# Fillers behind the band's scores, mixing in parts, rotation tables begun earlier and column norms in a transformer kernel

## The chip, the cores and the metric

The kernel runs on one core of a Trainium2 chip. Its time is device microseconds of one launch, and lower is better. TensorE (PE) multiplies, VectorE (DVE), ScalarE (ACT) and GpSimd (POOL) do elementwise work, SyncE (SP) starts the loads. The engines run their own queues in order and wait for each other by semaphores. TensorE's clock is granted at one of two levels, 1.2 GHz (0.50 in the views) and 2.4 GHz (1.00).

## The reference

512 tokens of width 1024 pass through two blocks. The first adds a mixer, a memory attention and an expert layer to the stream; the second (two layers, with a state-space mixer, a latent attention and a delta rule) is touched by the change only in its latent attention. The mixer, cut to what matters:

```python
proj = rmsnorm(h, norm_mix_g) @ w_in            # q, k, v of 8 heads of 64, and u
att = chunked_attention(rmsnorm(q), rmsnorm(k), v, rel_bias)
ssm = s5_mixer(u, ...)                          # x_t = a * x_{t-1} + B u_t, a = mag * exp(i * angle)
mixed = concat(rmsnorm(att, att_out_g), rmsnorm(ssm, ssm_out_g))
h = h + mixed @ w_out
# memory attention: k = rmsnorm(memn @ w_mem_k) per head of 256
```

Chunks of 64 queries see up to eight chunks of keys before them and their own, with a bias by distance. The state-space part is computed with tables of cos and sin of (angle x t) for all 512 t, `Er` and `Ei`, and a scan.

## The kernel before

Everything is float32. Activations lie transposed, 128 rows of a feature chunk by 512 tokens. Weight products are done as three products of a high and a low part (lines 103 to 105); `Weights` (line 430 on) loads a 128x1024 tile of weights, ScalarE makes its high part (L471), VectorE its low part (L483) two tiles ahead. `linears` runs a list of such products tile by tile; after tile i each engine also runs the step i of the norms given to it (`act_at`, `pe_at`, `dve_at`). `weights.filler` is a 128x128 tile of ones; `fill` (L458) issues products of it whose result nobody reads.

The first 0.7 ms run these stages in order, each closed by a barrier of all engines:

- mix_in (from 10 us): 16 tiles of w_in give q, k, v, u, with `GroupNorm` for q and k beside them (reciprocal of 128x512 on VectorE, L319) and `StateTables` on GpSimd, which computes the powers of the rotation (L1288 to 1292) and later, behind a small reciprocal of VectorE (L1266), the scaled C matrices. A turn of v (L809) follows.
- band attention (`attention`, L883; called at L1133): 32 jobs, 8 heads h by 4 blocks q of 128 queries, a job having (q+1) x 128 keys. In iteration j TensorE multiplies the scores of job j (L943), transposes the probabilities of job j-2 (L919), and, once a head's four jobs are turned, mixes the values of a whole head in one go (L932; L928 in the packed form of the latent attention), in iteration 4h+6. VectorE adds the bias (L973), takes the maximum (L976), and normalises job j-1 (L958, L962). ScalarE takes the exponential (L1009), copies the turned probabilities of j-2 (L995) and stores a head (L1000). GpSimd meanwhile doubles the rotation tables (`rotations`, L1322): from n known columns to 2n, for k = 0 to 8; in the last doubling ScalarE makes half the products (`act_aside`, L1341) in jobs 19 to 26, and waits at job 19 until k = 0 to 7 are done.
- state_space: 16 tiles, VectorE rotates and scans (L1398 to 1409), GpSimd rotates back (L1422 to 1425), both reading `Er` and `Ei`.
- gated unit, then mix_out: 8 tiles of w_mem_k and 8 of w_out. `GroupNorm` normalises the mixed stream (2 groups of 4 chunks) for the w_out tiles and the memory's k (4 groups of 2). For a group: squares (ACT), sums of the chunks (DVE, L315), one product with the tile of ones (PE, L304) that sums over rows and gives the sum on every row, root (ACT, L289), reciprocal (DVE, L319) and scaling (DVE, L322) over the whole width; then the high part (ACT, L294) and the low part (POOL, L327), for which the first w_out tile waits.
- mem_in, memory attention (L1183, two key tiles), mem_out, experts. Much later the latent attention runs twice (L2433), packed, with a gate's products between its jobs (`GateBeside`).

## Time and profile before

| | |
|---|---|
| time, median of 3 runs | 5266.63 us (5266.21 to 5267.07) |
| profiled execution, its own time | 5271.14 us |
| span of the profiled execution | 5269.4 us |
| TensorE busy | 4995.3 us (95%) |
| VectorE, ScalarE, GpSimd busy | 2956.7, 1774.7, 703.9 us (56%, 34%, 13%) |
| TensorE's granted clock, mean | 0.972 |

The profile lists one execution. Busy time of TensorE is modelled from pipelined products, so that differences of starts say more than durations. A row in order of time shows start, duration, engine, line, operation, output and inputs, a count where equal rows are merged, and in brackets the idle time before it with what ended it. A float32 product shows as two records.

### The profile page before, as it was taken

What the parts mean: (1) busy time and instruction counts of PE and PEld (TensorE: products, weight loads), DVE (VectorE), ACT (ScalarE), POOL (GpSimd) and SP (SyncE); (2) the same over time, 40 slices, a digit from 0 to 9 for tenths busy, and PEclk for the clock granted to TensorE, in tenths of its full rate; (3) what the DMA queues carried; (4) which work ended last, traced back from release to release, by engine and by line L of the source; (5) the groups of instructions that cost most, each with busy time, mean ns of one, the idle gap of its engine ahead of it and who ended that gap; (6) DMA issues with size and microseconds to landing.
All of it is one profiled execution on the core that took longest, in us unless ns stands there. A gap on an engine that the chain in (4) does not pass through costs nothing. (4 is left out here: it accounts for less than half of the span.)

```text
span 5269.4 us, 62000 instructions
## 1 busy us (share of the span) xinstructions
PE 4995.3 (95%) x23936; PEld 4012.4 (76%) x23936; DVE 2956.7 (56%) x5352; ACT 1774.7 (34%) x2720; POOL 703.9 (13%) x494
## 2 busy tenths in 40 slices
PE   8679899999999999999899998999999999989999
PEld 6227688888887888878887676888878876767887
DVE  6577558898403444465455465544565465566433
ACT  3314433333322322243333333343323333323422
POOL 3741002232240000001200001000003000011000
PEclk9799999999999999998999999999989999999999
DMA  2012123555546555530022020222210221212222
GB/s 105 24 42 86 53 103 118 184 185 185 182 152 217 192 192 192 195 113 24 1 96 84 33 88 32 104 96 96 90 43 1 83 70 56 72 45 96 92 98 82
DMA packets 231732, 527.57 MB, mean 100 GB/s; under 512 B 19600, under 2 KB 89488, under 8 KB 230032
## 3 DMA queue, kind: packets, MB, share of 16 engines
q1 hardware_dynamic: 231440, 523.61, 29.2%
q8 instruction: 192, 3.15, 0.2%
q14 instruction: 100, 0.82, 0.1%
HBM read 448.03 MB, written 75.50 MB: 99 GB/s over the span
## 5 line engine op out<-in xcount | busy, mean ns | idle before, releaser
L483 DVE TENSOR_TENSOR weight_low<-ring,weight_high 128x1024 fp32r<-128x1024 f32 (+2 forms) x606 | 710.4, 1173 | 1233.3 <-PE banks L105 1169.1
L471 ACT CAST weight_high<-ring 128x1024 fp32r<-128x1024 f32 (+2 forms) x728 | 729.1, 1003 | 540.8 <-PE banks L105 524.2
L103 PE MATMUL banks<-x_high,weight_high 128*128 128x512 f32 x1856 | 748.6, 403 | 30.0 <-DVE weight_low L483 17.0
L483 POOL TENSOR_TENSOR weight_low<-ring,weight_high 128x1024 fp32r<-128x1024 f32 x122 | 299.2, 2454 | 3302.9 <-PE banks L105 2146.6
L105 PE MATMUL banks<-x_high,weight_low 128*128 128x512 f32 x1856 | 728.8, 393 | 0.0
L104 PE MATMUL banks<-x_low,weight_high 128*128 128x512 f32 x1856 | 728.4, 392 | 0.0
L103 PEld LDWEIGHTS banks<-x_high,weight_high 128*128 128x128 f32 x1856 | 351.8, 190 | 143.2 <-issue 49.1
L103 PE MATMUL banks<-xn_high,weight_high 128*128 128x512 f32 x1024 | 411.0, 401 | 0.7 <-ACT hT L1638 0.7
L104 PEld LDWEIGHTS banks<-x_low,weight_high 128*128 128x128 f32 x1856 | 352.1, 190 | 75.4 <-issue 5.8
L105 PEld LDWEIGHTS banks<-x_high,weight_low 128*128 128x128 f32 x1856 | 351.4, 189 | 74.8
L103 PE MATMUL banks<-act_high,weight_high 128*128 128x512 f32 x1024 | 399.5, 390 | 5.6 <-DVE act_low L1870 5.6
L105 PE MATMUL banks<-xn_high,weight_low 128*128 128x512 f32 x1024 | 399.8, 390 | 0.0
L105 PE MATMUL banks<-act_high,weight_low 128*128 128x512 f32 x1024 | 399.1, 390 | 0.0
L104 PE MATMUL banks<-act_low,weight_high 128*128 128x512 f32 x1024 | 399.1, 390 | 0.0
L104 PE MATMUL banks<-xn_low,weight_high 128*128 128x512 f32 x1024 | 398.6, 389 | 0.0
L1841 ACT CAST act_high<-activations 128x512 fp32r<-128x512 f32 x126 | 78.8, 626 | 488.8 <-PE banks L105 484.9
L103 PEld LDWEIGHTS banks<-act_high,weight_high 128*128 128x128 f32 x1024 | 192.8, 188 | 46.4 <-issue 6.4
L105 PEld LDWEIGHTS banks<-xn_high,weight_low 128*128 128x128 f32 x1024 | 192.2, 188 | 41.5
L1749 DVE TENSOR_SCALAR first_hot<-iota,spare,rstd 128x128 f32<-128x128 f32 x512 | 185.2, 362 | 68.6 <-ACT rstd L1663 52.2
L104 PEld LDWEIGHTS banks<-act_low,weight_high 128*128 128x128 f32 x1024 | 192.8, 188 | 39.9
L105 PEld LDWEIGHTS banks<-act_high,weight_low 128*128 128x128 f32 x1024 | 192.7, 188 | 40.1
L103 PEld LDWEIGHTS banks<-xn_high,weight_high 128*128 128x128 f32 x1024 | 192.8, 188 | 36.1 <-ACT hT L1638 0.9
(616 smaller groups left out, 9127.5 us busy)
## 6 DMA issues: line engine op xcount, KB each, us to landing
ring<-in_peer_u SPq DMA_DIRECT2D x128, 512.0 KB, 3.4
ring<-in_peer_v SPq DMA_DIRECT2D x128, 512.0 KB, 3.4
acts<-dot_act SPq DMA_DIRECT2D x128, 256.0 KB, 2.0
gates<-gate_block SPq DMA_DIRECT2D x64, 512.0 KB, 6.1
ring<-in_w_up SPq DMA_DIRECT2D x64, 512.0 KB, 3.2
ring<-in_w_down SPq DMA_DIRECT2D x64, 512.0 KB, 3.2
activations<-acts SPq DMA_DIRECT2D x126, 256.0 KB, 3.7
gates_in<-gates SPq DMA_DIRECT2D x126, 256.0 KB, 3.9
```

The source lines that it names most:

```text
L103: nc.tensor.matmul(out, w_high, x_high, start=start, stop=False)
L104: nc.tensor.matmul(out, w_high, x_low, start=False, stop=False)
L105: return nc.tensor.matmul(out, w_low, x_high, start=False, stop=stop)
L471: self.nc.scalar.copy(self.wH[:, g % HIGHS, 0:kc * P], self.ring[:, g % SLOTS, 0:kc * P]).then_inc(self.high_made, 1)
L483: ops.tensor_tensor(self.wL[:, g % LOWS, 0:kc * P], self.ring[:, g % SLOTS, 0:kc * P], self.wH[:, g % HIGHS, 0:kc * P].bitcast(F32), ALU.s ...
L1749: v.tensor_scalar(hotA[:, m % HOTS, k, :], iota, first[:, n:n + 1], gateT[:, n:n + 1], ALU.is_equal, ALU.mult)
L1841: nc.scalar.copy(aH[:, n % 2, :], weighed_tile(n)).then_inc(act_high, 1)
```

## The change

1. **Fillers.** In each of the band's 32 jobs TensorE issues four products of the tile of ones into bank 7 behind the scores. Nobody reads them.
2. **Mixing in parts.** In all attentions a head's mixing is cut into parts (by key tile, or by query block in the packed form), one in each of the iterations from 4h+6 on. The store of a head moves back accordingly.
3. **Rotation tables.** The table is allocated before mix_in, as two halves of 256 columns. Doublings k = 0 to 5 are done by GpSimd in mix_in, right after the powers; 6 to 8 stay in the band attention. ScalarE's share of the last doubling moves from jobs 19 to 26 to jobs 13 to 20, with its wait. The input's high and low parts lie in the second half of the table until then; v's transpose moves into mixT and the tile of half-ones into vS. State_space reads both tables as 2 x 256 columns.
4. **Column norms.** mix_out's two norms become `ColumnNorm`: TensorE sums over rows with the data as weights and one column of ones, root and reciprocal are taken on 128 x 4 (or 128 x 2) elements, and TensorE spreads them over rows and columns with the identity. The scaling reads the result from PSUM. The first norm's groups follow each other one tile apart, no longer two.

The diff, cut to its core:

```diff
+class ColumnNorm(GroupNorm):
...
+        buffer, _, self.ident, columns, _ = tools
+        self.column, self.buffer, self.tiles = columns[:, 0:1], buffer, self.n // P
...
+    def root(self, g):
+        return self.buffer[:, g * self.tiles:(g + 1) * self.tiles]
...
+            self.nc.scalar.activation(self.root(g), self.bank(g)[:, 0:self.tiles], ACT.Sqrt, scale=1.0 / self.width, bias=self.eps)\
+                .then_inc(self.rooted, 1)
...
+    def pe_at(self, pe, i):
+        for g, chunks in self.at_step(i, 2):
+            pe.wait_ge(self.added, (g + 1) * (self.group - 1))
+            if g >= 3:
+                pe.wait_ge(self.scaled, (g - 2) * self.group)
+            for t in range(self.tiles):
+                last = self.nc.tensor.matmul(self.bank(g)[:, t:t + 1], self.scratch(chunks[0])[:, t * P:(t + 1) * P], self.column,
+                                             start=True, stop=True)
+            last.then_inc(self.summed, 1)
+        for g, chunks in self.at_step(i, 4):
+            pe.wait_ge(self.inverse, g + 1)
+            for t in range(self.tiles):
+                last = self.nc.tensor.matmul(self.bank(g)[:, t * P:(t + 1) * P], self.root(g)[:, t:t + 1].to_broadcast([P, P]), self.ident,
+                                             start=True, stop=True)
+            last.then_inc(self.spread, 1)
+
...
+        v = self.nc.vector
+        for g, chunks in self.at_step(i, 5):
+            dve.wait_ge(self.scaled, (g + 1) * self.group)
...
+        for g, chunks in self.at_step(i, 3):
+            dve.wait_ge(self.rooted, g + 1)
+            v.reciprocal(self.root(g), self.root(g)).then_inc(self.inverse, 1)
+        for g, chunks in self.at_step(i, 4):
+            dve.wait_ge(self.spread, g + 1)
+            for c in chunks:
+                v.scalar_tensor_tensor(self.y(c), self.x(c), self.gain(c), self.bank(g), ALU.mult, ALU.mult).then_inc(self.scaled, 1)
 
...
+MIXED_FROM = 6
+WARM = 4
+            def mix(h, part):
+                if part == 0:
+                    pe.wait_ge(copied, TT * (h + 1))
+                    if h >= 2:
+                        pe.wait_ge(stored, h - 1)
+                if packed:
+                    for k in range(part + 1):
+                        last = nc.tensor.matmul(banks[4 + h % 2][place(h), part * P:(part + 1) * P], values(h, k),
+                                                pt[:, h % 2, place_of(part) + k * P:place_of(part) + (k + 1) * P],
+                                                start=(k == 0), stop=(k == part))
+                elif part < keys(TT - 1):
+                    k = part
...
+            for j in range(len(jobs) + MIXED_FROM + TT):
...
+                    for _ in range(WARM if warm is not None else 0):
+                        nc.tensor.matmul(banks[7][:, 0:P], warm, warm, start=True, stop=True)
...
-                if j >= 3 and jobs[j - 3][1] == TT - 1:
-                    mix(jobs[j - 3][0])
+                h, part = divmod(j - MIXED_FROM, TT)
+                if 0 <= h < heads and part < parts:
+                    mix(h, part)
...
-                if j >= 4 and jobs[j - 4][1] == TT - 1:
-                    store(jobs[j - 4][0])
+                h, part = divmod(j - MIXED_FROM, TT)
+                if 0 <= h < heads and part == parts:
+                    store(h)
+                if 0 < h <= heads and parts == TT and part == 0:
+                    store(h - 1)
...
-                halves = mixT[:, 0, 0:P]
+                halves = vS[:, 2, 0:P]
...
+                vT = mixT[:, 0:4, :]
+                xH, xL = ssm.pair()
...
-                              aside=ssm, in_banks=True)
+                              aside=ssm, in_banks=True, warm=weights.filler)
...
-                    norm = GroupNorm(nc, chunks_of(mixT), chunks_of(mixT), 8, 4, tools, 512, lambda c: col("mixed_g", c), chunks_of(scratch),
-                                     banks, 0, 2, pair=pair)
+                    norm = ColumnNorm(nc, chunks_of(mixT), chunks_of(mixT), 8, 4, tools, 512, lambda c: col("mixed_g", c), chunks_of(scratch),
+                                      banks, 0, 1, pair=pair)
...
+        half = 4 * 2 * N * (T // 2)
+        self.x_at = [nc.sbuf_base + half + k * half // 2 for k in range(2)]
+        self.E = sb("turns", [P, 2, 2, N, T // 2])
+        self.first_half, self.second_half = self.E[:, 0], self.E[:, 1]
...
+        link(g.memset(self.first_half[:, 0, :, 0:1], 1.0))
+        link(g.memset(self.first_half[:, 1, :, 0:1], 0.0))
+        for k in range(self.EARLY):
+            self.double(g, link, k)
...
-    LAST = 8
+    EARLY, LAST, ACT_FROM = 6, 8, 13
...
+    def double(self, ops, link, k, before=None):
+        n, m = 1 << k, self.batch(k)
+        first = self.first_half
+        tmp = self.big[:, 0:m * n].rearrange("p (m n) -> p m n", n=n)
+        for t0 in range(0, SSM_TILES, m):
+            t = slice(t0, t0 + m)
+            c_, s_ = bc(self.power[:, k, 0, t], n), bc(self.power[:, k, 1, t], n)
+            if before:
+                before(t0 + m)
+            for which, op in ((0, ALU.subtract), (1, ALU.add)):
+                new = first[:, which, t, n:2 * n] if k < self.LAST else self.second_half[:, which, t, :]
+                link(ops.tensor_tensor(tmp, first[:, 1 - which, t, 0:n], s_, ALU.mult))
+                if k < self.LAST:
+                    link(ops.tensor_tensor(new, first[:, which, t, 0:n], c_, ALU.mult))
+                link(ops.tensor_tensor(new, new, tmp, op))
...
+        for k in range(self.EARLY, self.LAST):
+            self.double(ops, link, k)
+        self.double(ops, link, self.LAST, lambda tiles: eng.wait_ge(scaled, 2 * tiles))
...
+        k, j = self.LAST, j - self.ACT_FROM
+        if j == 0:
+            act.wait_ge(step, sum(6 * (SSM_TILES // self.batch(x)) for x in range(self.EARLY, k)))
+        for t in (2 * j, 2 * j + 1) if 0 <= j < SSM_TILES // 2 else ():
+            for which in range(2):
+                self.nc.scalar.activation(self.second_half[:, which, t, :], self.first_half[:, which, t, :], ACT.Copy,
+                                          scale=self.power[:, k, 0, t:t + 1]).then_inc(scaled, 1)
...
-                v.tensor_tensor(w[:, 0, :], b0, Er[:, i, :], ALU.mult)
...
+                v.tensor_tensor(w0, b0, Er(i), ALU.mult)
...
```

## Rows read from the trace of the kernel before

**Rows 1.** TensorE's rows in order of time, over one head of the band attention

```profile
145.50 1.12 PE L943 MATMUL banks<-qkT 64*128 64x512 f32 x2
...
148.85 0.55 PE L919 MATMUL banks<-ident,scratch 128*128 128x128 f32 x3 [1.44 <-DVE scratch L962]
...
150.23 0.66 PE L919 MATMUL banks<-ident,scratch 128*128 128x128 f32 x4 [0.20 <-DVE scratch L962]
...
152.32 3.56 PE L932 MATMUL banks<-ring,vS 128*64 128x512 f32 x8
155.81 1.12 PE L943 MATMUL banks<-qkT 64*128 64x512 f32 x2
156.86 0.44 PE L919 MATMUL banks<-ident,scratch 128*128 128x128 f32 x2
157.23 0.48 PE L943 MATMUL banks<-qkT 64*128 64x128 f32 x2
```

**Rows 2.** Busy time and count by engine, then PEclk, DMA share, GB/s, windows

```profile
149.50:152.00 2.50, 2.30 (x9) 0.92 (x9) 1.85 (x5) 2.25 (x7) 2.34 (x3) 0.87 0.00 0
152.00:154.50 2.50, 2.50 (x4) 0.85 (x5) 1.67 (x4) 0.92 (x4) 2.42 (x2) 0.50 0.01 3
154.50:157.00 2.50, 2.50 (x9) 1.00 (x8) 0.03 (x1) 0.00 (x0) 2.42 (x2) 0.95 0.00 0
```

**Rows 3.** ScalarE in the band attention, in order of time

```profile
168.72 0.69 ACT L1009 ACTIVATE banks<-scratch,spare 128x512 f32<-128x512 f32 x1 [4.29 <-DVE spare L976]
...
179.74 0.51 ACT L1348 ACTIVATE Er<-Er,power 128x256 f32<-128x256 f32 x1 [10.21 <-POOL Ei L1339]
...
219.61 0.69 ACT L1009 ACTIVATE banks<-scratch,spare 128x512 f32<-128x512 f32 x1 [4.65 <-DVE spare L976]
...
222.15 0.59 ACT L995 COPY ring<-banks 128x512 f32<-128x512 f32 x1 [0.62 <-PE banks L919]
...
226.89 0.58 ACT L1000 COPY mixT<-banks 64x512 f32<-64x512 f32 x1 [4.15 <-PE banks L932]
```

**Rows 4.** GpSimd in mix_in and the band attention, in order of time

```profile
105.61 0.22 POOL L1303 TENSOR_TENSOR ssm_par<-ssm_par 128x16 f32<-128x16 f32 x1 [38.29 <-DVE ssm_par L1266]
...
120.51 0.13 POOL L1325 MEMSET Er<- 128x16 f32 x1 [3.39 <-SPq L60]
...
141.55 1.90 POOL L1336 TENSOR_TENSOR scratch<-Ei,power 128x1024 f32<-128x1024 f32 x1
...
177.37 2.34 POOL L1339 TENSOR_TENSOR Ei<-Ei,scratch 128x1024 f32<-128x1024 f32 x1
```

**Rows 5.** VectorE and TensorE in mix_out, in order of time

```profile
402.12 3.35 DVE L319 RECIPROCAL scratch<-scratch 128x512 f32<-128x512 f32 x1
405.51 3.75 DVE L322 SCALAR_TENSOR_TENSOR mixT<-mixT,vec,scratch 128x512 f32<-128x512 f32 x4
409.18 2.29 DVE L483 TENSOR_TENSOR weight_low<-ring,weight_high 128x1024 fp32r<-128x1024 f32 x1
...
430.80 1.23 DVE L483 TENSOR_TENSOR weight_low<-ring,weight_high 128x1024 fp32r<-128x1024 f32 x1 [4.93 <-PE banks L105]
...
411.52 0.58 PE L103 MATMUL banks<-mem_high,weight_high 128*128 128x256 f32 x1 [5.27 <-DVE weight_low L483]
...
423.35 0.50 PE L103 MATMUL banks<-mixed_high,weight_high 128*128 128x512 f32 x1 [3.16 <-DVE weight_low L483]
```

**Rows 6.** Fillers at the end of mix_in; column sums in the last norm

```profile
113.75 2.17 PE L458 MATMUL banks<-ones 128*128 128x128 f32 x18
...
5255.36 1.95 PE L363 MATMUL banks<-columns,scratch 128*128 128x1 f32 x16 [1.38 <-DVE scratch L378]
```

**Rows 7.** TensorE in the memory attention and in the latent attention

```profile
571.64 0.44 PE L919 MATMUL banks<-ident,scratch 128*128 128x128 f32 x2 [0.35 <-DVE scratch L962]
571.91 1.03 PE L943 MATMUL banks<-qkT,mqT 128*128 128x256 f32 x4
...
2957.36 0.47 PE L103 MATMUL banks<-x_high,weight_high 128*128 128x512 f32 x1 [0.28 <-DVE gdn_v L855]
```

More of the change, by code:

```diff
@@ L933, in mix @@
                                             start=(k == 0), stop=(k == keys(TT - 1) - 1))
-                last.then_inc(mixed, 1)
-            for j in range(len(jobs) + 3):
+                if part == parts - 1:
+                    last.then_inc(mixed, 1)
+            for j in range(len(jobs) + MIXED_FROM + TT):
                 if j < len(jobs):
@@ L1000, in store @@
                 nc.scalar.copy(out(h), banks[4 + h % 2][place(h), :]).then_inc(stored, 1)
-            for j in range(len(jobs) + 4):
+            for j in range(len(jobs) + MIXED_FROM + TT + 1):
                 if j < len(jobs):
@@ L1127, in mix @@
+                linears(nc, "mix_in", [qk, Linear("mix_v", dram["w_in"], 8, 4, DC, x, scaled_to(vT, rstd)),
+                                       Linear("mix_u", dram["w_in"], 12, 4, DC, x, scaled_to(uT, rstd))],
+                        weights, banks, fold=fold, norms=[norm_qk, ssm], loads=ssm.loads)
+                turn(nc, "mix_v", chunks_of(vT), vS, 4, TT, banks, ident)
                 with tables:
[L1128 removed]
+                    ssm.turns(scratch)
```

120 lines of the change are left out of this document (56 added, 64 removed).

## The prediction

> **What bounds the kernel now.** The page first: TensorE is busy nearly throughout. So time can only be won where it waits, runs at the low clock, or does needless work, and everything the diff touches lies in the first 0.7 ms, apart from the order of the mixing in two later attentions. I read the stages there by windows, then engine by engine in order of time.
>
> The band attention (first scores just before 120.5 us, last copy out at 226.89 + 0.58 = 227.5) is the loose stage. One head is four jobs. In undisturbed stretches a head takes 155.81 - 145.50 = 10.31 us [rows 1]: VectorE and ScalarE have room, and TensorE loses 1.44 + 0.20 us waiting for normalised scores, and some more because its clock falls. The three windows that cover a head show a granted clock of 0.87, 0.50 and 0.95 [rows 2], so 2 x (0.13 + 0.50 + 0.05) x 2.5 = 3.4 us are at 1.2 GHz, which costs half of that, 1.7 us. The fall comes after a stretch with waits, and the long mixing product (3.56 us) then runs mostly at the low level [rows 1]. On top of that stands a stall: ScalarE waits 10.21 us for GpSimd's rotation tables, and the three heads from exponential 19 to exponential 31 take 219.61 - 168.72 = 50.9 us instead of 30.9 [rows 3]. GpSimd is the engine behind it: it starts at 120.51, and finishes the doublings k = 0 to 7 at 177.37 + 2.34 = 179.71 [rows 4].
>
> In mix_out the second bound shows: TensorE waits 5.27 and 3.16 us for weight_low, while VectorE does reciprocals of 3.35 us and scalings of 3.75 us ahead of it in its queue [rows 5].
>
> **Part 1, the doublings moved to the projection stage.** The six early ones took 141.55 - 120.51 = 21.0 us [rows 4] and now run inside mix_in, where GpSimd is idle for 38.29 us ahead of 105.61 [rows 4]. That idle time hides them; without it they would cost their 21 us. What remains before ScalarE may scale is k = 6 and 7: 179.71 - 141.55 = 38.2 us, so ready at 120.5 + 38.2 = 158.7 instead of 179.7. The last doubling (about 35 us) ends near 199, off the path. Price in mix_in: VectorE's subtraction L483 takes 1.23 us alone and 2.29 us beside GpSimd [rows 5], so up to 1.06 us for each of the three or four that meet the moved work, 4 us of delay at most, some of it regained, and the stage ends with GpSimd's chain behind VectorE's small reciprocal. Between 0 and 3 us; I take 0.5, because a product needs its weights only a tile later.
> The Trainium skill, "SBUF — State Buffer", section "SBUF: two separate sides", speaks against this move: a VectorE operation with two SBUF inputs and a GpSimd operation that reads SBUF exclude each other for a whole instruction. The 2.29 against 1.23 us agrees. If it held for every subtraction and every scaling beside the moved work, with none of it regained, the kernel would end 2.5 us later than I say.
>
> **Part 2, fillers and spread mixing in the band.** Each of 32 jobs gets four products of ones. Nine such products take 2.17 us [rows 6], 0.24 each with the last one's drain, so 16 a head cost about 3.7 us at the full clock. A head's other work at the full clock is 10.31 - 1.64 (waits) - 1.7 (low clock) = 7.0. So a head would take 7.0 + 3.7 = 10.7 us, with no wait left and the clock held: the fillers cost what the clock gives, and the steady pace does not improve (between 10.0, if switches between kinds of product overlap, and 11.3, if each filler group adds 0.15 us of switching; two transposes hold the next scores up for 157.23 - 156.86 = 0.37 us here and for 571.91 - 571.64 = 0.27 in the memory attention, so a switch can cost 0.1 and more [rows 1, 7]). The gain of the stage is the stall's. Walk: mixing is about 2.2 of the 10.7 and trails the scores by six jobs. Exponential 19 starts after five heads without mixing (5 x 8.5, less 1.5 that follows its scores) plus 3.4 heads' mixing (7.4), plus 1.4 on VectorE: 120.5 + 41.0 + 7.4 + 1.4 = 170.3; exponential 31 at 170.3 + 3 x 10.7 = 202.4, against 219.61 [rows 3].
> ScalarE reaches its wait at job 13 near 155 by the same count, so a stall of some 4 us stays; queued behind it are ScalarE's copies of turned probabilities, for which TensorE's transposes and mixing wait. Two jobs of slack absorb part of it, a fall of the clock in it costs something back: 0 to 6 us, I take 2.5. ScalarE's 16 scalings a head, at most 0.51 us each [rows 3], beside its own 3.2 us in 7.5 [rows 2], keep it at the same 10.7 us or slightly above for two heads. Exponential 31 then stands at 205. The tail was 7.9 us (219.61 to 227.5), with its mixing at the low clock; I take 7, so the stage ends at 212: **-15 us** (-8 to -21).
>
> **Part 3, ColumnNorm in mix_out.** Sums become one column and the inverse root is taken on 128x4 and spread by TensorE. VectorE loses two reciprocals of 3.35 us and four of half the width. Its scalings read the root from PSUM and no longer two SBUF tensors: 3.75 us for four becomes about 3.0. TensorE pays: 8 column products took 1.95 us [rows 6], so 4 cost 1.0, and four spreading products 4 x 0.24 = 1.0, against 0.9 for one product with ones: +1.1 for each of two wide groups and +0.55 for each of four narrow ones, 4.4 us. Walk: tile 2 still waits for the first sums to about 392. The four scalings of the first group, now behind a reciprocal and done at 409.2, run from about 403.8 to 407; the next subtraction follows a tile's end directly, so the 5.27 us wait goes, with the low clock behind it. Pace 1 instead of 2 brings the second group forward: scaled near 412.5, weight_low for the first w_out tile near 414.5 instead of 423.3 (TensorE starts at 423.35). That tile ended at 430.80 [rows 5], and now ends near 420.5, the wide groups' extra included. Gain 10, less the narrow groups' 2.2 in a stretch where TensorE never waits: **-8 us** (-3 to -11).
>
> **Part 4, spread mixing elsewhere.** In the memory attention TensorE waits 0.35 us a head at one place and about 0.7 in all [rows 7], because VectorE sat idle during the long mixing. Halved mixing removes part: 8 x 0.25 = -2 (0 to -5). In the latent attention, twice, 0.28 us a head is waited for the gate's eviction [rows 7]; a part of the mixing falls in front of it. That is 16 x 0.28 = 4.5 us to win, against three more switches a head of up to 0.15 us each, 7 us: -4.5 to +7, I take -2, since the wait has a row of its own there and a switch has none.
>
> **Part 5, the tables in two halves.** State_space reads Er and Ei as 2 x 256. VectorE sets its pace with 96 such operations. If every second piece cost 0.15 us this would be 14 us; on ScalarE a copy in four pieces takes 0.59 us and one in one piece 0.58 [rows 3], so I take 0.5 us, bounds 0 to 3. Smaller moves (the half-ones, vT, x in the second half) issue the same instructions: 0.
>
> **Sum.** 0.5 - 15 - 8 - 2 - 2 + 0.5 = -26. The profiled execution took 5271.14 (span 5269.4), the runs' median is 5266.63, 4.5 lower; the terms are taken off either: 5245 profiled, **5240 us** as median.
>
> **Rivals.** *The stall only moves (0.20).* ScalarE's wait comes at job 13 instead of 19 and TensorE's gap drops the clock; until it rises the fillers cost double, and ScalarE's scalings keep it behind. Then the band gives 5 us and mix_out 5: 5266.6 - 14 = 5252. For: in the old kernel the clock was low for the whole stretch after the stall. Against: 4 us of wait are not 10.
> *TensorE was the tighter bound in less than I think (0.10).* Switches overlap and the steady head takes 10.0: 7 x 0.7 = 5 us more gain, mix_out 10 and the latent attention 4.5: 5230.
> *The fillers are a tax (0.05, slower).* If the clock does not hold, the 16 fillers take 7.4 us a head and the rest 8.7 or more. Place: the band. With a share x of TensorE's work at the low clock a head takes 10.7 (1 + x) and the band 6 + 85.6 (1 + x), against 107 now (x = 0 gives my 92). It eats the band's own gain from x = 0.18 and, with the 11 us won elsewhere, the kernel's from x = 0.31. At a half it is 27 us over, in sum 5266.6 + 27 - 11 = 5283. For: a third of each head is at the low level today. Against: that third follows waits, and behind fillers there are none.
> *The moves cancel (0.06).* Switches at 0.15 us everywhere and two-piece access at a cost: 5263.
>
> **Chances and range.** Forecast case 0.59. Faster by over 0.2% (10.5 us, about what a measurement of this kernel can tell from no change) needs 5256.1 or less: 0.59 + 0.10 and 0.17 of the 0.20, so 0.86; within 0.2%: the other 0.03 and the last case's 0.06, so 0.09; slower: 0.05. The range takes in the first two rivals and the bounds of the band: 5226 to 5256.
>
> **What would show it.** GpSimd's doublings up to k = 5 before 90 us; ScalarE's wait for the tables under 6 us and near 155; heads at 10.4 to 11 us with a granted clock of 1.00 and no wait of TensorE between; the band over near 212 after a start at 120.5; no reciprocal of 3.35 us and no 5 us gap in mix_out; a first w_out tile ending about 10 us earlier relative to the stage's start; state_space as long as before. The prediction is wrong if the granted clock in the band stays below 0.9, if a head's period is over 11.3, or if mix_in or state_space lengthens by more than 3 us.

## The result, and the profile after

The changed kernel takes **5229.91 us** (median of 4 runs, 5220.98 to 5234.31), the kernel before, beside it, 5266.85 us (5266.21 to 5268.06): a ratio of 0.9931, 95% interval 0.9915 to 0.9946. Forecast were 5240 us and a range of 5226 to 5256. The profiled execution took 5234.31 us (span 5231.9) against 5271.14: 36.8 us less, where the sum said 26. On another chip the same kernel gave 5238.26 us, ratio 0.9935 [0.9921, 0.9949]. Its runs spread over 13 us on the first chip and 10 us on the second.

Where the time went, stage by stage. The times are those between first products of TensorE in the two traces (for the second latent attention, between the last product on mla_cq_high and the last on mla_y_high); the last column is the range over those later runs whose code in that stretch is the changed kernel's.

| stretch | before | after | gain | predicted | same code in later runs |
|---|---|---|---|---|---|
| up to the band's first scores | 120.47 | 120.56 | -0.1 | -0.5 | 119.4 to 120.8 |
| band attention | 107.3 | 98.5 | 8.8 | 15 | 95.6 to 101.0 |
| state_space | 131.0 | 129.4 | 1.6 | -0.5 | 129.3 to 132.1 |
| mix_out, to first product on mixed_high | 48.8 | 37.9 | 10.9 | 10 | 37.8 to 39.2 |
| from there to mem_in | 51.8 | 52.7 | -0.9 | -2.2 | 52.6 to 52.8 |
| memory attention | 65.1 | 61.0 | 4.1 | 2 | 60.9 to 61.1 |
| mem_out | 51.1 | 49.8 | 1.3 | 0 | 48.3 to 49.9 |
| gated delta stage (first product on act_high to that on gdn_y_high) | 1186.0 | 1182.0 | 4.0 | 0 | 1181.7 to 1189.4 |
| first latent attention (from mla_cq_high to mla_y_high) | 205.0 | 199.3 | 5.8 | 1 | 198.3 to 201.1 |
| second latent attention | 214.8 | 210.4 | 4.4 | 1 | 208.4 to 211.1 |

The gains listed make 39.9 us. The span became 37.5 us shorter, so the stretches not listed, which the change doesn't touch, took 2.4 back. The rows of before that answer to the ones below are [rows 1 to 5].

**The band attention.** ScalarE in order of time (start, duration, engine, line, operation, tiles, shape, and in brackets the idle time before it and who ended it); the 128x512 exponentials are those of every fourth job:

```profile
137.77 0.69 ACT L1090 ACTIVATE banks<-scratch,spare 128x512 f32<-128x512 f32 x1 [2.66 <-DVE spare L1057]
...
148.88 0.69 ACT L1090 ACTIVATE banks<-scratch,spare 128x512 f32<-128x512 f32 x1 [2.18 <-DVE spare L1057]
...
158.89 1.70 ACT L1448 ACTIVATE turns<-turns,power 128x256 f32<-128x256 f32 x4 [4.82 <-POOL turns L1433]
...
166.57 0.69 ACT L1090 ACTIVATE banks<-scratch,spare 128x512 f32<-128x512 f32 x1 [2.55 <-DVE spare L1057]
...
179.17 0.69 ACT L1090 ACTIVATE banks<-scratch,spare 128x512 f32<-128x512 f32 x1 [0.59 <-DVE spare L1057]
...
212.49 0.69 ACT L1090 ACTIVATE banks<-scratch,spare 128x512 f32<-128x512 f32 x1 [2.05 <-DVE spare L1057]
...
218.17 0.58 ACT L1081 COPY mixT<-banks 64x512 f32<-64x512 f32 x1 [1.98 <-PE banks L1009]
```

A steady head takes 148.88 - 137.77 = 11.11 us, and 30.9 us for three had become 50.9 around the old stall [rows 3]. The wait for GpSimd's table now comes at job 13 and is 4.82 us; but the two heads across it take 179.17 - 148.88 = 30.3 us instead of 22.2. The windows (busy time and count by engine, then granted clock, DMA share, GB/s) say where the 8 us go:

```profile
142.00:152.00 10.00, 10.00 (x54) 5.94 (x53) 5.88 (x15) 4.57 (x13) 9.69 (x5) 1.00 0.01 2
152.00:162.00 10.00, 5.33 (x28) 3.28 (x29) 2.93 (x8) 3.71 (x11) 6.62 (x4) 0.80 0.00 1
162.00:172.00 10.00, 10.00 (x36) 5.28 (x35) 3.71 (x9) 7.08 (x20) 8.35 (x4) 0.69 0.00 0
172.00:182.00 10.00, 10.00 (x56) 6.06 (x54) 6.14 (x16) 8.66 (x24) 9.61 (x6) 1.00 0.01 2
```

TensorE is busy 10.00 of 10 us at a clock of 1.00 before and after, and idle for 4.7 us in the second window. The clock falls in that idle time and comes back only behind it: 2 x (0.20 + 0.31) x 10 = 10.2 us are at the low level. About 3 of them lie in the idle time itself; in the other 7 TensorE is busy at 1.2 GHz, and half of them, 3.6 us, are lost. 4.7 + 3.6 = 8.3 us is the loss seen between the two heads. The fillers cost 1.0 us a job (147.32 to 148.32):

```profile
146.27 1.12 PE L1021 MATMUL banks<-qkT 64*128 64x512 f32 x2
147.32 1.16 PE L1026 MATMUL banks<-ones 128*128 128x128 f32 x8
148.32 0.38 PE L993 MATMUL banks<-ident,scratch 128*128 128x128 f32 x2
```

**GpSimd** does its early doublings from 63.87 to 89.66 us and has the table at 156.51 + 2.34 = 158.85, to 0.2 us as forecast:

```profile
63.87 0.23 POOL L1430 TENSOR_TENSOR vS<-turns,power 128x16 f32<-128x16 f32 x1
...
105.68 0.22 POOL L1399 TENSOR_TENSOR ssm_par<-ssm_par 128x16 f32<-128x16 f32 x1 [12.09 <-DVE ssm_par L1358]
...
156.51 2.34 POOL L1433 TENSOR_TENSOR turns<-turns,scratch 128x1024 f32<-128x1024 f32 x1
```

**mix_out**, VectorE and then TensorE: a reciprocal of 0.17 us stands where 3.35 us stood [rows 5], four scalings take 2.69 us, the spread 1.05, and TensorE begins on mixed_high with no wait in brackets. The 5.27 us wait is gone too; one wait of 5.19 us, for the sums in front of the first column products at 381.68, remains.

```profile
389.54 0.17 DVE L460 RECIPROCAL roots<-roots 128x4 f32<-128x4 f32 x1
...
393.39 2.69 DVE L464 SCALAR_TENSOR_TENSOR mixT<-mixT,vec,banks 128x512 f32<-128x512 f32 x4
...
408.97 1.22 DVE L552 TENSOR_TENSOR weight_low<-ring,weight_high 128x1024 fp32r<-128x1024 f32 x1 [4.42 <-PE banks L105]
...
391.56 1.05 PE L444 MATMUL banks<-ident,roots 128*128 128x128 f32 x8
...
402.03 0.50 PE L103 MATMUL banks<-mixed_high,weight_high 128*128 128x512 f32 x1
```

### The profile page after: what moved, and what is told of

The parts are those of the page before. It is cut to its first block and busy times, and to the rows that moved or that the text cites. A ratio compares the mean times of both kernels' runs of the same rounds, so it can differ in the third digit from the quotient of the medians.

```text
span 5231.9 us, 62616 instructions
## 1 busy us (share of the span) xinstructions
PE 5004.0 (96%) x24244; PEld 4033.3 (77%) x24244; DVE 2953.9 (56%) x5352; ACT 1775.5 (34%) x2720; POOL 710.4 (14%) x494
## 5 line engine op out<-in xcount | busy, mean ns | idle before, releaser
L104 PEld LDWEIGHTS banks<-xn_low,weight_high 128*128 128x128 f32 x1024 | 192.8, 188 | 35.3
```

The source lines that it names most:

```text
L104: nc.tensor.matmul(out, w_high, x_low, start=False, stop=False)
```

## The experiments

Every time is the median of its runs; "ratio" is to the kernel before on the same chip. "Band" is the time between the band's first scores and state_space's first product.

**No fillers, one, two.**

```diff
-WARM = 4
+WARM = 0
```

With 1 and 2 in its place in the next two.

> The changed kernel with no filler products in the band attention (four become zero); all else stays. Reading of its trace on which this rests: in the steady heads TensorE is busy 11.1 of 11.1 us at a granted clock of 1.00, and each group of four fillers takes 1.0 us, so a head is 7.1 us of own work and 4.0 of fillers. Theory A (the fillers only give back what they cost, as the prediction said of the steady pace): without them waits return, the granted clock falls to about 0.83 as in the kernel before, and a head takes 10.0 to 10.6 us. The start of ScalarE's scaling stays tied to GpSimd's table at 158.9, so only heads after it count: 4 x 0.8 = 3 us less, the kernel's median 3 us below the changed kernel's (0 to 6). Rival B (the fillers are a tax): the clock holds above 0.95 without them because the spread mixing already fills the gaps, a head takes 8.7 to 9.2, and the kernel ends 8 to 11 us earlier. Rival C (the fillers are what wins): a head takes over 11.2 us and the kernel is 3 us or more slower than the changed one.

> The changed kernel with one filler product a job instead of four. If the clock is held by the mere absence of waits (theory A with a threshold somewhere between none and four), a head takes 7.1 + 4 x 0.25 = 8.1 us of TensorE's work, but VectorE and ScalarE with their hand-overs need about 8.7 to 9.2, so waits of 0.6 to 1.1 us a head return; the clock then decides: 9.0 us a head if it holds at 1.00, 10.3 if it falls to 0.85. Theory A expects 9.8 to 10.4 and the kernel 3 us faster than the changed one; rival B (tax) 9.0 and 8 us faster; rival C (fillers win) over 11.2 and slower.

> The changed kernel with two filler products a job instead of four. TensorE's work in a head is 7.1 + 8 x 0.25 = 9.1 us, about what VectorE and ScalarE with their hand-overs need, so hardly any wait should stand. Theory A (the clock follows the waits): clock 0.97 or more, 9.1 to 9.5 us a head; ScalarE reaches its wait for the table 4 to 5 us earlier and waits that much longer (9 us instead of 4.8), and the heads after it are 4 x 1.8 = 7 us shorter: the kernel 5 to 8 us faster than the changed one. Rival B (tax) says the same here, and differs only at zero and one. Rival C: less filler, lower clock, no gain.

Measured: 5241.50 us (ratio 0.9946 [0.9933, 0.9960]), 5253.46 us (0.9965 [0.9951, 0.9979]) and 5233.48 us (0.9925 [0.9912, 0.9939]). Theory A and the rival of the tax both fall, and rival C holds by the trace; in the kernel's time the intervals of the first and of the changed kernel overlap. Without fillers (exponentials and windows):

```profile
180.19 0.69 ACT L1090 ACTIVATE banks<-scratch,spare 128x512 f32<-128x512 f32 x1 [1.73 <-DVE spare L1057]
...
193.57 0.69 ACT L1090 ACTIVATE banks<-scratch,spare 128x512 f32<-128x512 f32 x1 [3.11 <-DVE spare L1057]
```

```profile
182.00:192.00 10.00, 10.00 (x19) 3.27 (x17) 3.92 (x11) 5.72 (x17) 9.61 (x6) 0.50 0.00 1
192.00:202.00 10.00, 10.00 (x24) 4.34 (x24) 5.49 (x14) 3.19 (x9) 6.53 (x3) 0.50 0.00 0
```

A head takes 13.38 us at a clock of 0.50, from the first heads to 4 us before the band's end; the kernel before, with its waits, took 10.31 at 0.83 or so. TensorE is never idle in these windows and the clock still does not rise. At half speed TensorE is busy throughout and every other engine waits for it, so nothing else speeds the head up. Why a TensorE that shows busy does not get its clock back is not shown. It is not the missing fillers alone: the kernel before had none either, and with its mixing in one block each fall in a steady head lasted only 3.4 us [rows 2]. No run has the block, no fillers and the early tables together. One filler shows both levels in one trace:

```profile
155.15 0.69 ACT L1090 ACTIVATE banks<-scratch,spare 128x512 f32<-128x512 f32 x1 [3.77 <-DVE spare L1057]
...
170.67 0.69 ACT L1090 ACTIVATE banks<-scratch,spare 128x512 f32<-128x512 f32 x1 [2.05 <-DVE spare L1057]
...
203.53 0.69 ACT L1090 ACTIVATE banks<-scratch,spare 128x512 f32<-128x512 f32 x1 [1.51 <-DVE spare L1057]
...
212.15 0.69 ACT L1090 ACTIVATE banks<-scratch,spare 128x512 f32<-128x512 f32 x1 [1.39 <-DVE spare L1057]
```

```profile
142.00:152.00 10.00, 10.00 (x25) 4.59 (x24) 3.90 (x11) 3.50 (x10) 9.61 (x6) 0.50 0.00 0
202.00:212.00 10.00, 10.00 (x41) 4.70 (x40) 7.57 (x18) 4.46 (x14) 1.18 (x1) 1.00 0.00 0
```

15.52 us a head at 0.50, 8.62 at 1.00. So at the full clock the filler's price is as computed (2.49 us a head for three fillers in each of four jobs, 0.21 each), and the level of the clock decides more than that. The runs of one filler spread over 17 us; falls of different length would explain it, but only one of the five, the fastest, was traced. With two fillers a head at 1.00 takes 9.32 us (208.93 to 218.25), as computed, but the clock fell twice and the band took 105.1 us.

**ScalarE's scalings two jobs later.**

```diff
-    EARLY, LAST, ACT_FROM = 6, 8, 13
+    EARLY, LAST, ACT_FROM = 6, 8, 15
```

> The changed kernel with ScalarE's scalings begun beside job 15 instead of job 13, four fillers as there. In the changed kernel ScalarE waits 4.8 us for the table at 158.9, TensorE stands idle from 157 to about 161 and runs at half clock to about 167, and exponentials 11 to 19 take 30.3 us where two heads take 22.2: 8 us lost, not the 2.5 predicted. Theory S (the stall is worth those 8 us, the fall of the clock included): job 15 is reached at about 160.5, after the table, so no wait, exponentials 11 to 19 take 22.2 to 23.5 us, the band ends 6 to 8 us earlier and so does the kernel. Rival L (most of the loss is ScalarE's own load, 16 scalings of up to 0.5 us a head beside its other work, which only moves): exponentials 11 to 23 still take over 37 us and the kernel gains 2 us or less. Rival M: the last doubling now ends later (GpSimd near 204 instead of 200) and still before the stage's end, so it costs nothing; if it does, the band's end follows GpSimd.

Measured: 5226.40 us, ratio 0.9919 [0.9905, 0.9932], band 90.9 us.

```profile
148.54 0.69 ACT L1090 ACTIVATE banks<-scratch,spare 128x512 f32<-128x512 f32 x1 [2.18 <-DVE spare L1057]
...
159.65 0.69 ACT L1090 ACTIVATE banks<-scratch,spare 128x512 f32<-128x512 f32 x1 [2.06 <-DVE spare L1057]
...
171.12 0.69 ACT L1090 ACTIVATE banks<-scratch,spare 128x512 f32<-128x512 f32 x1 [0.83 <-DVE spare L1057]
...
204.59 0.69 ACT L1090 ACTIVATE banks<-scratch,spare 128x512 f32<-128x512 f32 x1 [2.06 <-DVE spare L1057]
```

Exponentials 11 to 19 take 22.6 us instead of 30.3, exponential 31 comes 7.9 us earlier (0.3 of it brought along from the start), and the scalings add 0.4 us to a head. Theory S holds and L falls; GpSimd ends its last doubling at 199.9, well before the band's end, so it costs nothing (M). In the kernel's time the gain is within what two chips differ by (0.9919 against 0.9931 and 0.9935); in the trace of the stage it is plain.

**Both norms of mix_out as before.**

```diff
-                    norm = ColumnNorm(... banks, 0, 1, pair=pair)
+                    norm = GroupNorm(... banks, 0, 2, pair=pair)
-                    norm_mk = ColumnNorm(
+                    norm_mk = GroupNorm(
```

> The changed kernel with both norms of mix_out as in the kernel before (sums spread over all partitions by a product with ones, reciprocals of 128x512 and 128x256, pace 2). Theory N: the column norms are worth what mix_out gained, 10.2 us (from the stage's first filler to the first product of mem_in: 111.0 us before... measured as first product on mixed_high 48.9 against 37.9 us after that filler, and 0.9 us given back later by the narrow groups). So the first product on mixed_high comes 48 to 50 us after the filler, the 5 us wait of TensorE for weight_low behind the scalings returns, and the kernel is 9 to 11 us slower than the changed one. Rival: part of the gain came from ahead of the stage (weights there earlier, another clock); then it is 5 us or less.

Measured: 5242.53 us, ratio 0.9948 [0.9932, 0.9965]. From the stage's first filler (361.82) to mixed_high 48.9 us instead of 37.9, from there to mem_in 51.8 instead of 52.7: 10.1 us, theory N. The two waits are back:

```profile
398.86 0.58 PE L103 MATMUL banks<-mem_high,weight_high 128*128 128x256 f32 x1 [5.28 <-DVE weight_low L552]
...
410.69 0.50 PE L103 MATMUL banks<-mixed_high,weight_high 128*128 128x512 f32 x1 [3.15 <-DVE weight_low L552]
```

**The mixing as one block in the memory and the latent attentions.**

```diff
+                if warm is None:
+                    for part in range(parts if j >= 3 and (j - 3) % TT == TT - 1 else 0):
+                        if (j - 3) // TT < heads:
+                            mix((j - 3) // TT, part)
+                    continue
                 h, part = divmod(j - MIXED_FROM, TT)
...
+                if warm is None:
+                    if j >= 4 and (j - 4) % TT == TT - 1 and (j - 4) // TT < heads:
+                        store((j - 4) // TT)
+                    continue
```

> The changed kernel with the mixing of a head as one block again in the memory attention and in both latent attentions; the band keeps its spread mixing and its fillers. Theory X: the spread gave the 4.1 us of the memory attention (first score to the first product on mem_y_high 65.1 us before, 61.0 after) and about 6 and 4 us of the two latent ones (first score to the first product on mla_y 131.2 against 124.7 us in the first), where the prediction gave 2 and 2: so 65, 131 and the kernel 12 to 15 us slower than the changed one. Rival V: the latent attentions' share is the same difference between executions as the 3.9 us that the untouched delta stage shows; then only the memory attention's 4 us return and the latent ones stand at 125.

Measured: 5247.42 us, ratio 0.9960 [0.9946, 0.9974]. The memory attention takes 65.2 us, mem_out 51.0; the latent ones 203.4 and 214.3, against 198.3 to 201.1 and 208.4 to 211.1 in all runs with the spread. So the spread is worth 4.2 + 1.1 + about 4 + about 3.5 = 13 us, and the kernel's time agrees (0.9960 against 0.9931 and 0.9935). Theory X; the prediction had 4.

**No early doublings.**

```diff
-    EARLY, LAST, ACT_FROM = 6, 8, 13
+    EARLY, LAST, ACT_FROM = 0, 8, 19
```

> The changed kernel with no doubling in the projection stage (all of k = 0 to 7 by GpSimd in the band, ScalarE's scalings from job 19 as before); four fillers and the spread mixing stay. Theory P: GpSimd has its table at 179.7 as in the kernel before; ScalarE reaches job 19 at about 171.6 (128.4 + 4 heads of 11.1 - 1.2), waits some 8 us, and the idle TensorE and the fall of its clock cost another 3, so exponential 31 stands near 216 to 218 against 212.5 and the kernel is 3 to 6 us slower than the changed one. So the early tables are worth 4 us with the wait at job 13, and about 12 with it at job 15. Rival Q: the stall now lies as far behind as before and costs 10 us or more, kernel 10 slower. Rival R: the doublings beside mix_in cost something there that their return gives back: mix_in more than 1 us shorter.

Measured: 5236.27 us, ratio 0.9939 [0.9922, 0.9955]; the wait at job 19 is 7.62 us (179.45), the band 100.0 us, against 98.5 and 99.8 for the changed kernel (and 95.6 and 101.0 in the two other traces of the same band code). So the move of the doublings, with ScalarE's wait at job 13, is worth 0 to 1.5 us by the first two and can't be told from nothing by all four, less than the 3 to 6 expected: one stall with its fall of the clock was exchanged for another of about the same price (9.2 us over the head from 171.02 to 191.35). With the wait at job 15 the same move is worth 100.0 - 90.9 = 9.1 us. Mix_in is no shorter (mix_x_high's last product at 113.1 in both): rival R falls.

This run also shows what fillers and spread mixing do in the band by themselves, since its tables are as late as before:

```profile
171.02 0.69 ACT L1090 ACTIVATE banks<-scratch,spare 128x512 f32<-128x512 f32 x1 [2.18 <-DVE spare L1057]
...
213.93 0.69 ACT L1090 ACTIVATE banks<-scratch,spare 128x512 f32<-128x512 f32 x1 [2.05 <-DVE spare L1057]
```

Exponential 19 comes 2.3 us later than in the kernel before (168.72), because a steady head takes 11.11 us and not 10.31. From there to exponential 31 it is 42.9 us instead of 50.9 [rows 3]. The band is 107.3 - 100.0 = 7.3 us shorter, and all of it is won behind the stall: TensorE stands idle for 5.8 us there and not 11.2, and has its full clock again after 10.2 us, where windows of 10 us from 172 on showed 0.50, 0.50, 0.67, 0.80 and 0.83 in the kernel before. How this divides between fillers and spread no run tells.

**The mixing as one block in the band alone.** The same diff with `if warm is not None`.

> The changed kernel with the mixing of a head as one block again in the band attention alone, four fillers as they are. Without fillers and with spread mixing the granted clock was 0.50 in the whole band and a head took 13.4 us; with four it was 1.00 and a head 11.1. This run asks whether the fillers hold the clock alone. Theory F (they do; the spreading of the mixing is worth little once no wait is left): clock 0.97 or more, head 11.1 to 11.6, kernel within 4 us of the changed one. Rival G (both are needed): behind the block of mixing VectorE has had nothing for 2 us, TensorE waits for normalised scores, the clock falls below 0.85 in part of every head and a head takes over 12.5: the kernel 8 us or more slower.

Measured: 5237.68 us, ratio 0.9943 [0.9926, 0.9959], band 99.0 us.

```profile
190.67 0.69 ACT L1095 ACTIVATE banks<-scratch,spare 128x512 f32<-128x512 f32 x1 [4.20 <-DVE spare L1062]
...
201.34 0.69 ACT L1095 ACTIVATE banks<-scratch,spare 128x512 f32<-128x512 f32 x1 [3.96 <-DVE spare L1062]
...
212.02 0.69 ACT L1095 ACTIVATE banks<-scratch,spare 128x512 f32<-128x512 f32 x1 [3.95 <-DVE spare L1062]
```

10.68 us a head at a clock of 1.00: four fillers hold the clock without the spread, and the head is even 0.4 us shorter than with it. Where ScalarE scales beside it, though, heads take 10.8 to 13.0 us, against 11.3 and 11.5 with the spread (171.12 to 182.38, and 159.65 to 171.12 in the run from job 15). Theory F for the steady heads. The spread's own worth in the band isn't settled, since this execution had its fall of the clock at the start (0.50 from 122 to 132) and no stall at the table. It had a gap of TensorE, though, behind ScalarE's late copies, and the clock stayed at 1.00 through it:

```profile
173.97 2.26 PE L1009 MATMUL banks<-ring,vS 128*64 128x512 f32 x7 [2.18 <-ACT ring L1081]
```

**The changed kernel again; four fillers, then one or none.**

```diff
-                    for _ in range(WARM if warm is not None else 0):
+                    for _ in range((WARM if j < 8 else 1) if warm is not None else 0):
-    EARLY, LAST, ACT_FROM = 6, 8, 13
+    EARLY, LAST, ACT_FROM = 6, 8, 17
```

The first of the three is the changed kernel, unaltered; the third has 0 where the second has 1.

> The changed kernel once more, unaltered, beside the next two on one chip, and as a second look at what varies between executions. Its own band took 98.5 us in the first trace, and 95.6 and 101.0 us in two kernels whose band is the same code: with a stall of 4.8 us the clock falls to 0.50 for 10 us and more, with a stall that scheduling made shorter it does not fall. Expected: 5226 to 5236 us, band between 95 and 101 us, heads without stall 11.1 us, state_space 129.3 to 132.1 us (so that the 1.6 us between the first two traces there is nothing of the change), the gated delta stage 1181 to 1190 us.

> The changed kernel with four fillers in the first eight jobs and one in each later job, and ScalarE's scalings from job 17, which at the faster pace is reached near 159. With one filler throughout, a head took 15.5 us at a granted clock of 0.50 until 182 us and then 8.6 us at 1.00. Theory H (the clock keeps the level it has; the fillers are needed where waits would let it fall, not behind that): the clock is at 1.00 throughout, heads after the second take 8.6 to 8.8 us, the band ends 98.5 - 6 x 2.4 = 84 us after its start, or at GpSimd's last product near 200 (80 us) if that is later, and the kernel is 10 to 15 us faster than the changed one: about 5216. Rival T (a head needs its four fillers all the time, and the end of the one-filler run was chance): the clock falls to 0.50 within two heads of job 8, heads take 15.5 us, and the kernel is 10 us or more slower.

> The same with no filler at all after the eighth job. Without any filler a head took 13.4 us at a granted clock of 0.50 in the whole band, and its own work on TensorE at 1.00 is 7.1 us, below the 8.6 that the hand-overs between the engines need, so that waits of about 1.5 us a head must stand. Theory H in its strong form (the level is kept by itself) gives clock 1.00 and 8.6 us a head, like the run with one filler. Theory W (the clock falls once waits stand, and holds only while TensorE has none): the clock falls by the third or fourth head, heads of 10 to 13.4 us, kernel slower than the run with one filler by 10 us or more.

Measured: 5238.26 us (ratio 0.9935), band 99.8; 5235.33 us (0.9931 [0.9918, 0.9945]), band 99.7; 5228.69 us (0.9922 [0.9909, 0.9936]), band 95.9. The last, exponentials of ScalarE and two waits of TensorE:

```profile
146.06 0.69 ACT L1090 ACTIVATE banks<-scratch,spare 128x512 f32<-128x512 f32 x1 [1.34 <-DVE spare L1057]
...
154.24 0.69 ACT L1090 ACTIVATE banks<-scratch,spare 128x512 f32<-128x512 f32 x1 [1.21 <-DVE spare L1057]
...
206.74 0.69 ACT L1090 ACTIVATE banks<-scratch,spare 128x512 f32<-128x512 f32 x1 [3.11 <-DVE spare L1057]
...
154.98 0.55 PE L993 MATMUL banks<-ident,scratch 128*128 128x128 f32 x3 [0.66 <-DVE scratch L1043]
...
161.03 1.97 PE L1009 MATMUL banks<-ring,vS 128*64 128x512 f32 x2 [2.25 <-ACT ring L1076]
```

With no filler at all a head takes 8.18 us at 1.00, waits of 0.66 us included. Theory W said that these would bring the clock down; in the two heads before the scalings they don't. The fall comes with the gap of 2.25 us at 161, behind ScalarE's copies, which are late behind its scalings; from there to 212 every window shows 0.50, and a head takes 13.4 us. With one filler it is the same: 8.6 us a head, a gap of 2.18 us ahead of 178.11, then 15.5 us. Neither H nor T nor W is right as written. The level survived small waits, and in these two traces it was lost at the first gap of over 2 us. The length of the gap isn't the whole rule: the run with block mixing and four fillers kept 1.00 through one of 2.18 us.

**Fillers only where another engine is late.**

```diff
-                    for _ in range(WARM if warm is not None else 0):
+                    for _ in range((WARM if j < 8 or 16 <= j < 27 else 1) if warm is not None else 0):
-    EARLY, LAST, ACT_FROM = 6, 8, 13
+    EARLY, LAST, ACT_FROM = 6, 8, 17
```

> The changed kernel with four fillers beside jobs 0 to 7 and 16 to 26 and one beside each other job, and ScalarE's scalings from job 17. The last two traces showed that a head needs 8.2 to 8.6 us at a granted clock of 1.00 with one filler or none, and that the level was lost at the first gap of over 2 us, when ScalarE's copies came late behind its scalings (a wait of 2.2 us at 158 and 176). Theory W (the fillers are needed only where another engine is late, at the start and beside the scalings): clock 1.00 throughout; exponentials at 137.5, 146, 155, then 166 and 178 beside the scalings with their fillers, 187 and 195.5 for the last, the band's end near 201, where GpSimd's last product also ends, so the band takes 81 us instead of 98.5 and the kernel's median is 5216 to 5222, 4 to 10 us below the one with the scalings moved alone. Rival Z (the level is lost anyway at the first scalings, because TensorE arrives earlier there than the table): the band takes 95 us or more and the kernel 5228 or more.

Measured: **5223.50 us** (4 runs, 5216.85 to 5227.36), ratio 0.9911 [0.9894, 0.9927], band **82.9 us**, 15.6 less than the changed kernel's and 24.4 less than before's.

```profile
147.12 0.69 ACT L1090 ACTIVATE banks<-scratch,spare 128x512 f32<-128x512 f32 x1 [1.51 <-DVE spare L1057]
...
155.74 0.69 ACT L1090 ACTIVATE banks<-scratch,spare 128x512 f32<-128x512 f32 x1 [1.39 <-DVE spare L1057]
...
177.43 0.69 ACT L1090 ACTIVATE banks<-scratch,spare 128x512 f32<-128x512 f32 x1 [0.60 <-DVE spare L1057]
...
188.53 0.69 ACT L1090 ACTIVATE banks<-scratch,spare 128x512 f32<-128x512 f32 x1 [2.18 <-DVE spare L1057]
...
197.15 0.69 ACT L1090 ACTIVATE banks<-scratch,spare 128x512 f32<-128x512 f32 x1 [1.39 <-DVE spare L1057]
```

Heads of 9.1 and 8.6 us, 10.4 to 11.3 beside the scalings, and 8.6 again, clock 1.00 throughout the band and no gap of TensorE over 0.9 us in it behind the first scores. Rival Z falls and theory W holds; its band (81 us said) and its median (5216 to 5222 said) were each missed by under 2 us. It was the lowest median of all, and 14 us of its gain at the first product on act_high (1560.9 against 1574.7) were still there; in the profiled execution 7 of them went in the gated delta stage, which took 1188.9 us there and 1182.0 in the changed kernel's, with the same code. Over the kernel its interval overlaps that of the run with the scalings from job 15 and that of the changed kernel; what is plain is the band.

## Why the prediction was right, and where it was not

**What bounds the kernel.** Right: all gains lie where TensorE waited or ran slow.

**Part 1, mix_in.** 0.5 us predicted, 0.1 measured. GpSimd's six doublings grew from 21.0 to 25.8 us beside VectorE's work and found room in its idle time. The rule of the Trainium skill that the prediction weighed ("SBUF — State Buffer", section "SBUF: two separate sides") would have made it 2.5 us more; the stretching is there, the delay is not: nearly all of it falls on GpSimd, which had 12 us left (12.09 us idle ahead of 105.68), while of VectorE's subtractions beside it two grew, to 1.35 and 2.07 us.

**Part 2, the band.** -15 predicted, -8.8 measured. *The head*: 10.7 said, 11.11 measured. A group of four fillers is 1.0 us and not 0.94, and the rest 7.1 and not 7.0. *The table*: 158.7 said, 158.85. *The stall*: this is the step that failed. Its wait was right (4 said, 4.82), its price was not: 2.5 said, 7.6 measured by the run that removes it (98.5 - 90.9; 8.9 from the second trace of the changed kernel). I let the slack of two jobs absorb part of the wait and put "a fall of the clock in it" into the bounds (0 to 6). In fact the slack absorbed next to nothing, 4.67 us of the 4.82 arrived at TensorE as idle time, and the clock was low for 10.2 us, 7 of them behind that idle time. Without the stall, exponential 31 stands at 204.6 (202.4 said), the tail is 6.3 us (7 said). Two of the prediction's own signs missed by this: heads at 10.4 to 11 us, and the band over near 212, where it was over at 218.8.

That the steady pace would not improve was right in its number, wrong in its reading. "The fillers cost what the clock gives" compared the new order with fillers to the old order without. With the mixing spread, the right comparison is the new order without fillers, and it takes 13.4 us a head, not 10.3. The fillers gave 2.3 us a head against that; but 4.0 us a head of them were needed only at some places. Against the kernel before, the changed one loses 0.8 us in each steady head, and the run with the block mixing and four fillers loses 0.4 (10.68). So the band's gain is the stall's, as said: it cost 50.9 - 30.9 = 20 us before [rows 3] and 30.3 - 22.2 = 8.1 now, 12 us less; six steady heads give 5 of them back, and the tail is 1.6 shorter.

**Part 3, ColumnNorm.** -8 predicted, -10.0 measured, and by undoing it 10.1. The walk was right (37.9 us to mixed_high, 11 less than before, 10 said). The narrow groups were mis-sized: 2.2 us said, 0.9 measured. The sign "no 5 us gap in mix_out" fails as worded, since the wait for the first sums stays (5.19 us); the walk had kept it.

**Part 4, the spread elsewhere.** -4 predicted, about -13 by the run that undoes it. Two steps failed. I took only part of the waits that had rows (0.25 of 0.7 us a head in the memory attention, and 0.28 in the latent one set against 7 us for switches). The switches cost nothing that can be seen: a steady head of the latent attention went from 15.11 us (2924.34 to 2939.45) to 14.79 (2919.83 to 2934.62), that is by more than its whole wait. And what follows a stage was left out: mem_out gained 1.1 to 1.3 us, because its first products run at the low clock for a shorter time. The first 15 us of mem_out before, after, in the run with the block mixing there, and in the second trace of the changed kernel:

```profile
623.20:638.20 15.00, 15.00 (x54) 12.11 (x55) 6.78 (x10) 5.40 (x9) 0.00 (x0) 0.80 0.27 99
...
598.60:613.60 15.00, 14.99 (x60) 12.25 (x61) 7.72 (x11) 5.84 (x9) 0.00 (x0) 0.90 0.27 101
...
607.00:622.00 15.00, 15.00 (x54) 12.14 (x55) 6.88 (x10) 5.51 (x9) 0.00 (x0) 0.81 0.26 97
...
601.10:616.10 15.00, 14.96 (x66) 12.41 (x67) 7.76 (x11) 5.88 (x9) 0.00 (x0) 1.00 0.36 131
```

The stage took 51.1, 49.8, 51.0 and 48.3 us. In the latent attentions the rows settle the rest: between the 128x512 exponentials of the first two heads lie 13.1 us in every trace with the spread and 15.1 without it, the later heads are 0.3 us shorter each, and the tail is 10.0 us in both. That is 2.0 + 6 x 0.3 = 3.9 us for each of the two. What comes on top in the first one is the start: its first 15 us had a clock of 0.66 before, 0.89 after and 0.77 with the block mixing, and that varies between executions of the same code.

**Part 5, tables in two halves.** 0.5 us predicted; state_space took 129.4 us against 131.0, and 129.3 to 132.1 in executions of the same code. Nothing is visible, as forecast.

**The sum.** 26 said, 36.8 measured. Against it the band gave 6 less, mix_out 2 more and the attentions elsewhere with mem_out 12 more, state_space 2 by chance, and 4 came in the gated delta stage, where the changed kernel's first trace is at the low end of 1181.7 to 1189.4. The first latent attention had luck too, about 2 us of its 5.8. So the total was nearer than its largest two terms: two errors of opposite sign met, which is luck.

**The rivals.** The stall that only moves (0.20) is close to what the band did (8.8 us gained, 5 in the rival; and by the run without early doublings the move was worth next to nothing), but it gave mix_out too little. (Its terms, 5 + 5 + 4 - 1, make 13 us and 5254, not 14 and 5252; and the clock of the old kernel, which it took to be low for the whole stretch after the stall, was back at 0.80 from 202 to 212.) The tax (0.05) is refuted from both sides: fewer fillers everywhere made the kernel slower or no faster. It asked at which share of low clock fillers lose, and missed that with the spread mixing fillers end the low clock. Where the clock is at 1.00 anyway they are a tax: 11.1 us a head against 8.6 and 8.2.

## What to carry to other kernels

Judge filler products against the same order without them and against the order they replace, and put them where another engine will be late (the first jobs, the stretch in which ScalarE has extra work), not beside every job. When a wait is moved or shortened, price the gap by what TensorE loses behind it: a wait of 4.8 us cost 7.6. Moving the producer earlier is worth little until the consumer's wait is gone altogether; here starting two jobs later gained the 8 us that the move alone did not bring. Not tested here: the early tables with the mixing in one block and no fillers.

## What the runs showed of the hardware

**With the mixing spread, the time at half speed after a fall tends to be shorter with more fillers, and TensorE's busy time doesn't tell it.** Time at the low level, added up from windows of 10 us as 2 x (1 - clock) x 10: with no filler about 100 and 55 us (back only 4 and 1 us before the band's end); with one 61 and 31; with two 17 and 38; with four 10.2, 10.2, 10.2, 10.4, 13.6, 13.6 and 13.6 us, in seven falls of six kernels. With the mixing in one block and no filler, as in the kernel before, it was 3.4 us in a steady head [rows 2], so the number of fillers isn't all that counts; which kinds of product bring the clock back was not tested one by one. In the windows at 0.50 that hold no gap TensorE was busy 9.8 to 10.0 of 10 us. The Trainium skill, "TensorE: Matmul & The Clock Gate", section "Part 1: The HAM clock gate", says that "the default state is throttled, and activity releases the throttle". The falls with four fillers agree; the run without any shows that activity cannot be read off the busy time of a profile: 10.00 of 10.00 us at 0.50.

**Falls in the middle of the band came with gaps of TensorE.** In the traces with the mixing spread, every fall past the first 5 us of the band and before its end began in a gap of 2.2 to 5.8 us or within 2 us behind one, and the traces without such a gap (the scalings from job 15, the placed fillers) had no fall. The reverse doesn't hold: one gap of 2.18 us passed without a fall. And in the kernel before, a wait of 1.44 us in each steady head was followed by a fall in each [rows 1 and 2].

**The same code falls in one execution and not in another.** With four fillers from the first job, the clock stood at 1.00 from 122 to 132 us in seven traces and at 0.50 or 0.51 in three. In one of the three (with the old norms) the fall delayed ScalarE so far that it reached its wait just as the table was ready, at 157.8: the band took 95.6 us, less than the 98.5 of the undisturbed start. The range of the band with the same code (95.6 to 101.0 us) and that of the gated delta stage (1181.7 to 1189.4 us) are together as large as the 13 us between runs of the changed kernel; only two of its nine runs were traced, so that they are its source is likely and not shown.
